# A two-layer diffusion backbone step: adaLN columns, W2 tile order, row splits and skewed output blocks

## The chip, the cores and the metric

The kernel runs on one core of a Trainium2 chip. The metric is the device time of one execution in microseconds (us). TensorE (PE) multiplies, VectorE (DVE), ScalarE (ACT) and GpSimd (POOL) do the elementwise work, and SyncE (SP) issues nearly all DMA transfers, in the order of its program.

## The reference

1152 tokens (1024 latent tokens and 128 context tokens) of width 1024 pass through two layers. Everything is float32.

```python
for i in range(2):
    sh1, sc1, g1, sh2, sc2, g2 = split(silu(cond) @ mod_w[i] + mod_b[i], 6)
    h = rmsnorm(x, norm1_g[i]) * (1 + sc1) + sh1
    if i == 0:    # gated short convolution
        bg, cg, xv = split(h @ sc_w_in, 3)
        y = (bg * dwconv3(cg * xv, conv_w, conv_b)) @ sc_w_out
    else:         # latent attention, 16 heads, with rotary keys and a context cache
        y = attention(h) @ mla_w_o
    x = x + g1 * y
    h = rmsnorm(x, norm2_g[i]) * (1 + sc2) + sh2
    x = x + g2 * (square(relu(h @ mlp_w1[i])) @ mlp_w2[i])
```

`cond` has two rows, one for the latent and one for the context tokens. It is the same for all tokens of its kind, so `mod` is a table of 96 columns (2 layers x 6 chunks x 8 tiles), each 128 x 2.

## The kernel before

Activations lie transposed: a tile is 128 channels x 1152 tokens, and `x`, `h_hi` and `h_lo` have eight tiles each. Every float32 operand is split into a high part (fp32r, a rounded copy) and a low part (the difference). `three` (line 845) makes each product as high x high, high x low and low x high, over three token blocks of 384 columns: nine matmuls for one tile of weights and one tile of rows.

A weight block is 128 x 1024. SP loads it into `w_raw`, ACT makes `w_hi` (line 532), POOL `w_lo` (line 459), in two slots that alternate. The high part of block b waits until PE has finished block b - 2. A stage is one output tile in three PSUM banks; there are two sets of banks, and `stage_free` counts how often one was read out. `stage` runs the eight tiles of one block. `skewed_blocks` runs two blocks in step, the second two tiles behind the first, so that PE has twice the work for each row tile as it comes. It is used behind a norm. `h_ready` makes PE wait for each low row tile.

The order of the work:

- Start. SP queues `vec`, `ident`, eight tiles of x, `mod_bias`, sixteen adaLN column tiles of 512 KB (`mod_first`), and then weight blocks (`load`) and adaLN rows (`load_mod`) in turn. PE copies the conditioning rows (`cond_rows`, line 913), makes columns 0 to 7 (`first_mod`, line 906), the sum of squares (lines 935 and 941) and columns 8 to 15. `first_mod_out` on DVE adds the bias. `norm` needs all sixteen: DVE scales x (line 1293), ACT adds the shift for the high part (line 562), DVE makes the low part (line 1305).
- Input blocks, 24 of them, three for each of eight channel tiles. DVE multiplies two outputs into `pad` (line 1422), filters it (lines 1428 and 1431) and multiplies by the third output (line 1439) into `v32`. In between it makes the next adaLN columns (`mod_next`, line 1241, two row products with an accumulator, and line 1244).
- `split_rows` on ACT (line 570) makes the high rows of `v32`, all eight behind the last product. `low_rows` on DVE (line 1315) makes the low rows.
- `out_blocks`: eight output blocks in a loop of pairs. DVE adds each to x (`residual`, line 1324), ACT squares, DVE adds the squares (line 1265).
- MLP: eight chunks. A chunk has four blocks of W1, each of which gives one hidden tile (ACT line 591, DVE line 1353, ACT line 594, DVE line 1358), and four blocks of W2. A W2 block gives two output tiles (halves) from four hidden tiles. PE runs half 0 over tiles 0 to 3 and then half 1. In the first W2 block (k == HT) half 0 waits for each hidden tile.
- Layer 1: latent projections, then eight pairs of heads. A step (`STEPS` is 19 for a head) is `scores` on PE, the exponential on ACT (line 767), its high part on ACT (line 769), its low part `p_lo` on POOL (line 475), `values` on PE. `over_sums` on DVE (lines 1664 and 1666) divides `o32` by the sums of a pair in five pieces. It does so in the middle of the next pair, and for the last pair behind it. The tiles `h_hi` and `h_lo` share memory with the latents and the heads' operands.
- Then `split_rows(o32)`, `low_rows`, the transfer that brings x back (queued on SP behind `sums_used`), `out_blocks`, norm, MLP.

Of the kernel before, what the change touches and what calls it, by code (L numbers as in the profile page):

```python
# [13 lines left out]
P = 128  # L14
# [36 lines left out]
SKEW = 2  # L51

# [96 lines left out]
def build(nc, T, outs):  # L149
    y_t, new_ckv, new_kpe = outs  # L150
    with ExitStack() as ctx:
# [30 lines left out]
        mod_acc = new("mod_acc", [P, 2, 2])  # L182
        gain = new("gain", [P, 4, KT, 2])
# [18 lines left out]
        mod_first0 = at("mod_first0", [P, KT, WSLOT], F32, G0)  # L202
# [8 lines left out]
        mod_first1 = at("mod_first1", [P, KT, WSLOT], F32, H0 + KT * N * 4)  # L211
# [56 lines left out]
        mod_prod = ps[:, 6 * BANK:8 * BANK]  # L268

# [16 lines left out]
        mf_loaded = [sem(f"mf_loaded{s}") for s in range(FIRST_MODS)]  # L286
# [25 lines left out]
        h_lo_done = sem("h_lo_done")  # L312
        relu_done = sem("relu_done")
# [33 lines left out]
        def _(sp):  # L347
# [24 lines left out]
            for j in range(KT):  # L372
                sp.dma_start(x[:, j, :], T["x_t"][:, j, :]).then_inc(x_loaded[j], 16)
            sp.dma_start(mod_bias[:, :], T["mod_bias"]).then_inc(const_in, 16)
            for m in range(FIRST_MODS):
                tile = (mod_first0, mod_first1)[m // KT]
                sp.dma_start(tile[:, m % KT, :], T["mod_cols"][m]).then_inc(mf_loaded[m], 16)
# [7 lines left out]
            load_in(0, 0)  # L385
# [132 lines left out]
        def _(act):  # L518
# [48 lines left out]
            def split_rows(src):  # L567

                for j in range(KT):
                    act.activation(h_hi[:, j, :], src[:, j, :], ACT.Copy).then_inc(h_hi_done, 1)  # L570

# [47 lines left out]
            act.wait_ge(row_mm, 1)  # L619
            act.activation(cond_row[:, :, :].rearrange("p c n -> p (c n)"), ps[:, 0:2 * D], ACT.Copy).then_inc(row_out, 1)  # L620

            def x_tile(j):
                act.wait_ge(x_loaded[j], 16)
                return x[:, j, :]

            rms(x_tile, KT, D)
            split_hi()
            split_hi()
            norm(0, 0, False)

            def in_blocks():

                for k in range(6):
                    if k % 3 == 0:
                        act.wait_ge(stage_done, L.count("s", 1))
                        act.wait_ge(stage_free, L.count("s"))
                        act.activation(cols3(tmp[0][:, 0:N]), stage_ps(L.at["s"]), ACT.Copy).then_inc(stage_free, 1)
                    L.at["s"] += 1
                    split_hi()

            with act.Fori(0, KT // 2) as i:
                L.enter(i, b=6, s=6)
                in_blocks()
                L.leave(KT // 2)
            act.wait_ge(stage_free, L.at["s"])
            split_rows(v32)
# [3 lines left out]
            if LAYERS > 1:  # L650
# [177 lines left out]
                act.wait_ge(sums_used, 3 + 3 * PAIRS)  # L828
                split_rows(o32)
# [6 lines left out]
        def _(pe):  # L836
# [11 lines left out]
            def stage(w0, tiles, src, ready=None):  # L848
# [5 lines left out]
                for k in range(tiles):  # L854
                    if ready:
# [4 lines left out]
                                [lambda t, r=r: r[:, k, t * TB:(t + 1) * TB] for r in src])  # L860
                ins.then_inc(stage_done, 1)
# [28 lines left out]
            def h_block(ready=None):  # L890
                weights()
                stage(lambda k: k * P, KT, (h_hi, h_lo), ready)
# [5 lines left out]
            def first_mod(m):  # L898

                b = 6 + m % 2  # L900
                raw = (mod_first0, mod_first1)[m // KT][:, m % KT, :]
                pe.wait_ge(mf_loaded[m], 16)
                if m >= 2:
                    pe.wait_ge(mod_done, m - 1)
                for k in range(KT):
                    ins = pe.matmul(bank(b, 2), raw[:, k * P:(k + 1) * P], cond[:, k, :], start=k == 0, stop=k == KT - 1)
# [38 lines left out]

            def chunk(behind_norm=None):
# [3 lines left out]
                for k in range(2 * HT):  # L950
                    if k < HT:
                        if not (behind_norm and k < 2):
                            h_block()
                    else:
                        weights()
                        for half in range(2):
                            def hid_ready(t):
                                pe.wait_ge(hid_lo_done, L.count("hid", -t - 1))
                            stage(lambda t: t * 2 * P + half * P, HT, (hid_hi, hid_lo),
                                  hid_ready if k == HT and half == 0 else None)  # L960
# [24 lines left out]
            with pe.Fori(1, KT // 2) as i:  # L985
# [3 lines left out]
                L.leave(KT // 2 - 1)  # L989
            C["h"] = KT  # L990

            def out_blocks():
                with pe.Fori(0, KT // 2) as i:
                    L.enter(i, b=2, s=2)
                    for k in range(2):
                        h_block(h_ready(C["h"]) if k == 0 else None)
                    L.leave(KT // 2)
# [220 lines left out]
        def _(dve):  # L1218
# [9 lines left out]
            def first_mod_out(m):  # L1228

                dve.wait_ge(mod_mm, m + 1)  # L1230
                dve.tensor_scalar(mod[:, m, :], bank(6 + m % 2, 2), mod_bias[:, m:m + 1], None,
                                  ALU.add).then_inc(mod_done, 1)
                L.at["m"] += 1

# [33 lines left out]
            def inverse_root():  # L1268
# [5 lines left out]
                dve.wait_ge(stage_free, L.at["s"])  # L1274
# [35 lines left out]
            def low_rows(dst, src, hi, n):  # L1310

                for j in range(n):
# [81 lines left out]
            for j in range(KT):  # L1394
                add_square(j % 2)
                first_mod_out(j)
            inverse_root()
            for m in range(KT, FIRST_MODS):
                first_mod_out(m)
            norm(0, 0, False)  # L1400
# [9 lines left out]
            with dve.Fori(0, KT // 2) as i:  # L1410
                L.enter(i, s=6, m=6)
                S.enter(i, n=12)
                for f in range(2):
                    mod_next(i * 6 + (FIRST_MODS + 3 * f))
                    L.at["s"] += 1

                    dve.wait_ge(stage_done, L.count("s", 1))
                    dve.wait_ge(stage_free, L.count("s"))
                    dst = [pad[:, 1:1 + 2 * TB].rearrange("p (t n) -> p t n", t=2),
                           pad[:, 1 + 2 * TB:1 + NS], pad[:, NS + 3:N + 3]]  # L1420
                    for o, (v, g, _) in zip(dst, parts(L.at["s"], tmp[0])):
                        ins = dve.tensor_tensor(o, v, g, ALU.mult)
                    ins.then_inc(stage_free, 1)
                    L.at["s"] += 1
                    mod_next(i * 6 + (FIRST_MODS + 3 * f + 1))
                    dve.wait_ge(stage_free, L.count("s"))
                    col = [vec[:, ds(i * 2 + (taps + w * KT + f), 1)] for w in range(3)]
                    own(dve.tensor_scalar(tmp[2][:, 0:W2], pad[:, 0:W2], col[0],
                                          vec[:, ds(i * 2 + (bias0 + f), 1)], ALU.mult, ALU.add))
                    for w in (1, 2):  # L1430
                        own(dve.scalar_tensor_tensor(tmp[2][:, 0:W2], pad[:, w:w + W2], col[w], tmp[2][:, 0:W2],
                                                     ALU.mult, ALU.add))

                    dve.wait_ge(stage_done, L.count("s", 1))
# [381 lines left out]
```

## Time and profile before

| | |
|---|---|
| median of 3 runs | 3251.74 us (3251.46 to 3254.78) |
| profiled execution | 3250.7 us, span 3248.9 us |
| PE busy | 3053.8 us (94%) |
| DVE, ACT, POOL busy | 1478.2, 1009.9, 852.4 us |
| mean granted PE clock | 0.959 of full speed |

Times in the rows are microseconds from the start of the span. A line of the timeline gives start, duration, engine, line, operation, output and inputs, the count, and in brackets how long the engine had been idle and what ended that. The granted clock is either 1.0 (2.4 GHz) or 0.5 (1.2 GHz) at any moment; a stretch shows the mean.

### The profile page before, as it was taken

To read this page: it belongs to the slowest core of one execution; us is meant where nothing else is said; L and a number is where in the kernel's file an instruction comes from. 1 tells how busy PE (TensorE), PEld (TensorE's weight loads), DVE (VectorE), ACT (ScalarE), POOL (GpSimd) and SP (SyncE) were. 2 spreads that over 40 slices of the span, in tenths; PEclk is the share of its full clock that TensorE was granted. 3 is DMA by queue.
4 is the path that set the end of the run, shared out by engine and by line. 5 is a ranking of instruction groups with operands and counts; after the bars stand their busy time and mean duration, and the time that the engine had idled before them with its cause. 6 is when DMAs were issued, how large, how long until landed. Compare 5 with 4: busy or idle time off the path is not lost.

```text
span 3248.9 us, 43718 instructions
## 1 busy us (share of the span) xinstructions
PE 3053.8 (94%) x17193; PEld 2920.4 (90%) x17193; DVE 1478.2 (45%) x1856; ACT 1009.9 (31%) x1447; POOL 852.4 (26%) x509
## 2 busy tenths in 40 slices
PE   7999998999999999887999999999889999999999
PEld 7999998999999999886777787777789999999999
DVE  1654545555445555744566565665433222222222
ACT  2211213111111112222766677766422111111111
POOL 0121111221121211120544456545311112121211
PEclk6999998999999999886999999999989999999999
DMA  5222220222112221120000000000211111111112
GB/s 196 67 78 93 75 90 33 78 85 72 64 65 89 79 71 58 59 73 6 8 7 2 7 5 7 8 6 1 88 35 33 46 39 40 44 45 39 39 45 78
DMA packets 45532, 166.60 MB, mean 51 GB/s; under 512 B 5792, under 2 KB 7456, under 8 KB 45216
## 3 DMA queue, kind: packets, MB, share of 16 engines
q1 hardware_dynamic: 44912, 160.89, 14.2%
q10 hardware_dynamic: 560, 4.87, 0.4%
q8 instruction: 43, 0.70, 0.1%
q14 instruction: 17, 0.14, 0.0%
HBM read 156.15 MB, written 9.58 MB: 51 GB/s over the span
## 4 chain that ended last, share of the span: by engine, by line
PE 49%; issue 33%; POOL 12%; DVE 3%; ACT 2%; POOLq 0%; DVEq 0%; ACTq 0%
PE ps L845 48%; POOL p_lo L475 10%; POOL w_lo L459 2%; DVE tmp L1353 1%; DVE hid_lo L1358 1%; ACT hid_hi L594 1%; ACT tmp L591 1%; DVE x L1324 0%; DVE ps L1241 0%; PE ps L941 0%; ACT tmp L539 0%; PE ps L935 0%; DVE tmp L1265 0%; ACT p L767 0%; POOLq L474 0%
## 5 line engine op out<-in xcount | busy, mean ns | idle before, releaser
L459 POOL TENSOR_TENSOR w_lo<-w_raw,w_hi 128x1024 fp32r<-128x1024 f32 (+2 forms) x190 | 462.5, 2434 | 1978.0 <-ACT w_hi L532 1978.0
L845 PE MATMUL ps<-h_hi,w_hi 128*128 128x384 f32 x2640 | 607.4, 338 | 49.7 <-DVE h_lo L1305 24.8
L845 PE MATMUL ps<-h_lo,w_hi 128*128 128x384 f32 x2640 | 604.3, 336 | 0.0
L845 PE MATMUL ps<-h_hi,w_lo 128*128 128x384 f32 x2640 | 603.5, 336 | 0.0
L845 PEld LDWEIGHTS ps<-h_hi,w_hi 128*128 128x128 f32 x2640 | 474.4, 190 | 54.1 <-issue 43.7
L532 ACT ACTIVATE w_hi<-w_raw 128x1024 fp32r<-128x1024 f32 (+2 forms) x190 | 194.6, 1025 | 984.3 <-PE ps L845 912.1
L475 POOL TENSOR_TENSOR p_lo<-p,p_hi 128x512 fp32r<-128x512 f32 (+1 forms) x304 | 381.7, 1270 | 375.9 <-ACT p_hi L769 372.5
L845 PEld LDWEIGHTS ps<-h_lo,w_hi 128*128 128x128 f32 x2640 | 475.2, 190 | 0.0
L845 PEld LDWEIGHTS ps<-h_hi,w_lo 128*128 128x128 f32 x2640 | 474.5, 189 | 0.0
L1324 DVE SCALAR_TENSOR_TENSOR x<-ps,mod,x 128x256 f32<-128x256 f32 (+5 forms) x432 | 240.1, 612 | 480.2 <-PE ps L845 478.6
L845 PE MATMUL ps<-hid_hi,w_hi 128*128 128x384 f32 x1536 | 350.4, 335 | 9.7 <-DVE hid_lo L1358 9.6
L845 PE MATMUL ps<-hid_lo,w_hi 128*128 128x384 f32 x1536 | 348.8, 334 | 0.0
L845 PE MATMUL ps<-hid_hi,w_lo 128*128 128x384 f32 x1536 | 348.7, 334 | 0.0
L1353 DVE SCALAR_TENSOR_TENSOR tmp<-ps,tmp 128x1152 f32<-128x1152 f32 x64 | 86.9, 1358 | 494.4 <-ACT tmp L591 494.4
L845 PEld LDWEIGHTS ps<-hid_hi,w_hi 128*128 128x128 f32 x1536 | 272.5, 188 | 15.1 <-DVE hid_lo L1358 14.7
L845 PEld LDWEIGHTS ps<-hid_hi,w_lo 128*128 128x128 f32 x1536 | 273.8, 188 | 0.0
L845 PEld LDWEIGHTS ps<-hid_lo,w_hi 128*128 128x128 f32 x1536 | 273.7, 188 | 0.0
L1646 DVE TENSOR_REDUCE row_max<-ps 128x1 f32<-128x1152 f32 x144 | 178.1, 1237 | 155.5 <-PE ps L1118 155.5
L591 ACT ACTIVATE tmp<-ps 128x1152 f32<-128x1152 f32 x64 | 72.6, 1135 | 531.7 <-PE ps L845 531.7
L767 ACT ACTIVATE p<-ps 128x512 f32<-128x512 f32 (+1 forms) x304 | 175.7, 578 | 119.5 <-PE ps L845 111.3
L1241 DVE CUSTOM_DVE_ANT_0 ps<-mod_raw,cond_row 128x1024 f32<-128x1024 f32 x80 | 211.6, 2645 | 1.6 <-issue 0.7
L769 ACT ACTIVATE p_hi<-p 128x512 fp32r<-128x512 f32 (+1 forms) x304 | 187.0, 615 | 9.7
(135 smaller groups left out, 3567.1 us busy)
## 6 DMA issues: line engine op xcount, KB each, us to landing
w_raw<-in_wall_dram SPq DMA_DIRECT2D x174, 512.0 KB, 3.7
mod_raw<-in_mod_rows_dram SPq DMA_DIRECT2D x80, 512.0 KB, 3.5
mod_first<-in_mod_cols_dram SPq DMA_DIRECT2D x16, 512.0 KB, 15.0
x<-in_x_t_dram SPq DMA_DIRECT2D x8, 576.0 KB, 7.4
x_spill<-x ACTq DMA_DIRECT2D x1, 4608.0 KB, 15.3
x<-x_spill SPq DMA_DIRECT2D x1, 4608.0 KB, 13.5
out_dram<-x SPq DMA_DIRECT2D x8, 576.0 KB, 2.8
w_raw<-in_wall_dram SPq DMA_DIRECT2D x8, 416.0 KB, 3.1
```

Of the source, the lines that this page charges most:

```text
L459: pool.tensor_tensor(w_lo[s][:, 0:words], w_raw[s][:, 0:words], w_hi[s][:, 0:words].bitcast(F32), ALU.subtract).then_inc(w_lo_done, 1)
L475: pool.tensor_tensor(p_lo[s][:, 0:n], p32[s][:, 0:n], p_hi[s][:, 0:n].bitcast(F32), ALU.subtract).then_inc(p_lo_done, 1)
L532: act.activation(w_hi[s][:, 0:words], w_raw[s][:, 0:words], ACT.Copy).then_inc(w_hi_done, 1)
L591: act.activation(cols3(tmp[0][:, 0:N]), stage_ps(L.at["s"]), ACT.Relu).then_inc(relu_done, 1)
L594: act.activation(hid_hi[:, k, :], tmp[1][:, 0:N], ACT.Copy).then_inc(hid_hi_done, 1)
L767: act.activation(p32[s][:, 0:n], bank(3 + pos % 2, n), ACT.Exp, scale=SCALE).then_inc(p_exp, 1)
L769: act.activation(p_hi[s][:, 0:n], p32[s][:, 0:n], ACT.Copy).then_inc(p_hi_done, 1)
L845: ins = pe.matmul(out, lhs[a], rhs[b](cols), start=first and n == 0, stop=last and n == 2)
L1241: ins = dve.tensor_tensor_reduce(product, raw, cond_row[:, c, :], 1.0, 0.0, ALU.mult, ALU.add, mod_acc[:, slot, c:c + 1])
L1324: ins = dve.scalar_tensor_tensor(xt, v, mod[:, ds(gate, 1), c:c + 1].rearrange("p a c -> p (a c)"), xt, ALU.mult, ALU.add)
L1353: dve.scalar_tensor_tensor(cols3(tmp[1][:, 0:N]), stage_ps(L.at["s"]), 0.0, cols3(tmp[0][:, 0:N]), ALU.max, ALU.mult).then_inc(stage_free, 1)
L1646: dve.tensor_reduce(row_max[:, t:t + 1], ps[:, 0:n], AX_X, ALU.max).then_inc(max_free, 1)
```

## The change

Four things are changed.

1. Start. Only the eight shift columns are made on PE (`first_shift`), three ahead of the sum of squares and five behind it. The scale columns come as rows (`scale_rows`) and are made on DVE as `mod_next` makes the later ones (`first_gain`, straight into `gain`). `mod_bias` is queued ahead of x. The column tiles, weight blocks 0 and 1 and the scale rows are queued among the tiles of x and behind them. ACT squares two tiles ahead of copying the conditioning rows, and splits weight blocks 0 and 1 ahead of the root.
2. `first_down_block` runs the first W2 block of each chunk in the order of `DOWN_ORDER`.
3. Convolution result: in the last input block PE signals `h_free` behind each tile of `h`, ACT splits `v32` tiles 0 to 6 behind these, and DVE makes their low rows ahead of the last product. Tile 7 follows behind it. Attention result: DVE makes the high rows of tiles 0 to 6 and the low rows of tiles 0 to 4 during the last pair, and the rest behind the sums. ACT does none of it.
4. `out_blocks` begins with `skewed_blocks` for its first two blocks, in both layers.

```diff
+ROWS_FREE = 5
+FIRST_SHIFTS, FIRST_GAINS = 3, 2
+DOWN_ORDER = [(0, 0), (0, 1), (0, 2), (1, 0), (1, 1), (0, 3), (1, 2), (1, 3)]
...
+            sp.dma_start(mod_bias[:, :], T["mod_bias"]).then_inc(const_in, 16)
...
+            for j in range(0, KT, 2):
+                load_x(j)
+                load_x(j + 1)
+                load_shift(j // 2)
+            load(0)
+            load(1)
+            for k in range(KT // 2):
+                load_scale(k)
+                load_shift(KT // 2 + k)
+            for k in range(KT // 2, KT):
+                load_scale(k)
...
-            load_in(0, 0)
+            load_mod(0)
+            load_mod(1)
+            load(2)
+            load_mod(2)
...
-            rms(x_tile, KT, D)
+                square(x[:, j, :], j % 2, D)
             split_hi()
             split_hi()
+            rms(None, 0, D)
+            act.wait_ge(mod_done, FIRST_MODS)
             norm(0, 0, False)
...
-            act.wait_ge(stage_free, L.at["s"])
-            split_rows(v32)
+            act.wait_ge(stage_free, L.at["s"] - 3)
+            for j in range(KT):
+                if j < KT - 1:
+                    act.wait_ge(h_free, j + 1)
+                else:
+                    split_hi()
+                    act.wait_ge(stage_free, L.at["s"])
+                act.activation(h_hi[:, j, :], v32[:, j, :], ACT.Copy).then_inc(h_hi_done, 1)
...
+            def first_down_block():
+
+                weights()
+                slot = L.at["b"] % 2
+                for half, t in DOWN_ORDER:
+                    if t == 0:
+                        pe.wait_ge(stage_free, L.count("s", 1 - half))
+                    if half == 0:
+                        pe.wait_ge(hid_lo_done, L.count("hid", -t - 1))
...
-            for m in range(KT):
-                first_mod(m)
+            for k in range(FIRST_SHIFTS):
+                first_shift(k)
             pe.wait_ge(row_out, 1)
             sum_squares(KT)
-            for m in range(KT, FIRST_MODS):
-                first_mod(m)
+            for k in range(FIRST_SHIFTS, KT):
+                first_shift(k)
...
             def out_blocks():
-                with pe.Fori(0, KT // 2) as i:
+                skewed_blocks(h_ready(C["h"]))
+                with pe.Fori(1, KT // 2) as i:
...
+            def first_gain(k):
+
+                dve.wait_ge(scale_loaded[k], 16)
+                raw, slot = mod_scale[:, k, :], k % 2
+                for c, product in enumerate((mod_junk[:, :], raw)):
+                    ins = dve.tensor_tensor_reduce(product, raw, cond_row[:, c, :], 1.0, 0.0, ALU.mult, ALU.add,
+                                                   mod_acc[:, slot, c:c + 1])
+                own(ins)
+                g0 = VEC["norm1_g"][0]
+                dve.tensor_scalar(gain[:, 0, k, :], mod_acc[:, slot, :], scale_bias[:, k:k + 1],
+                                  vec[:, g0 + k:g0 + k + 1], ALU.add, ALU.mult).then_inc(mod_done, 1)
...
+                for k in range(KT):
+                    if k == FIRST_GAINS:
+                        inverse_root(False)
+                    first_gain(k)
+                dve.wait_ge(stage_free, L.at["s"])
+                scaled(0)
+                shifts_out()
...
+                if last:
+                    low_rows(h_lo, v32, h_hi, 0, KT - 1)
+                dve.wait_ge(stage_done, L.count("s", 1))
...
+                def high_row(j):
+                    dve.tensor_copy(h_hi[:, j, :], o32[:, j, :]).then_inc(h_hi_done, 1)
+
                 pair(False, True, PAIRS - 2)
+                dve.wait_ge(sums_used, 3 * PAIRS)
+                for j in range(ROWS_FREE):
+                    high_row(j)
+                    low_rows(h_lo, o32, h_hi, j, j + 1)
+                for j in range(ROWS_FREE, KT - 1):
+                    high_row(j)
                 for piece in range(5):
                     over_sums(piece, PAIRS - 1)
                 dve.wait_ge(sums_used, 3 + 3 * PAIRS)
-                low_rows(h_lo, o32, h_hi, KT)
+                low_rows(h_lo, o32, h_hi, ROWS_FREE, KT - 1)
+                high_row(KT - 1)
+                low_rows(h_lo, o32, h_hi, KT - 1, KT)
```

## Rows read from the trace of the kernel before

**Rows 1.** The page, part 1: busy time, share and instructions of each engine.

```profile
PE 3053.8 (94%) x17193; PEld 2920.4 (90%) x17193; DVE 1478.2 (45%) x1856; ACT 1009.9 (31%) x1447; POOL 852.4 (26%) x509
```

**Rows 2.** Waits on PE: total us, times, the longest.

```profile
PE ps L845 <- DVE h_lo L1315: 19.1, 2, 11.4
```

**Rows 3.** Stretches: length, busy PE, PEld, DVE, ACT, POOL, clock, DMA share, GB/s.

```profile
16.00:22.10 6.10, 5.98 (x32) 5.98 (x32) 0.00 (x0) 0.00 (x0) 0.00 (x0) 1.00 1.03 410
...
55.70:80.40 24.70, 24.67 (x131) 24.58 (x129) 1.54 (x7) 3.02 (x3) 4.65 (x2) 0.56 0.07 22
...
581.03:681.76 100.73, 100.14 (x576) 99.82 (x576) 51.38 (x63) 17.25 (x16) 20.32 (x9) 1.00 0.21 74
...
2272.00:2289.00 17.00, 16.55 (x70) 12.60 (x69) 0.03 (x1) 15.89 (x29) 15.18 (x12) 1.00 0.00 0
...
2309.66:2315.10 5.44, 5.44 (x17) 5.44 (x18) 5.44 (x5) 5.44 (x6) 0.00 (x0) 0.51 1.00 434
```

**Rows 4.** Timeline of the start, up to the first DVE row products.

```profile
16.12 6.25 PE L913 MATMUL ps<-ident,cond 128*128 128x128 f32 x32 [16.12 <-DMA mod_bias<-in_mod_bias_dram]
...
52.16 3.78 PE L941 MATMUL ps<-ident,root 128*128 128x128 f32 x18 [0.61 <-DVE root L1272]
...
55.78 24.59 PE L906 MATMUL ps<-cond,mod_first 128*128 128x2 f32 x128
...
80.41 0.22 DVE L1231 TENSOR_SCALAR mod<-ps,mod_bias 128x2 f32<-128x2 f32 x1 [3.19 <-PE ps L906]
...
85.69 1.30 PE L845 MATMUL ps<-h_hi,w_hi 128*128 128x384 f32 x3 [5.32 <-DVE h_lo L1305]
...
105.90 1.23 DVE L1241 CUSTOM_DVE_ANT_0 ps<-mod_raw,cond_row 128x1024 f32<-128x1024 f32 x1 [0.28 <-DVE tmp L1406]
...
108.58 0.23 DVE L1244 TENSOR_SCALAR mod<-mod_acc,mod_bias 128x2 f32 x1 [0.30 <-DVE mod_acc L1241]
```

**Rows 5.** Timeline of the convolution seam.

```profile
385.13 1.42 DVE L1431 SCALAR_TENSOR_TENSOR tmp<-tmp,vec,tmp 128x1154 f32<-128x1154 f32 x1 [0.15 <-DVE tmp L1431]
...
388.94 1.49 DVE L1439 TENSOR_TENSOR v<-ps,tmp 128x768 f32 x3 [2.38 <-PE ps L845]
389.87 2.35 POOL L459 TENSOR_TENSOR w_lo<-w_raw,w_hi 128x1024 fp32r<-128x1024 f32 x1 [10.02 <-ACT w_hi L532]
...
394.84 10.24 DVE L1315 TENSOR_TENSOR h_lo<-v,h_hi 128x1152 fp32r<-128x1152 f32 x8
...
396.34 1.30 PE L845 MATMUL ps<-h_hi,w_hi 128*128 128x384 f32 x3 [7.64 <-DVE h_lo L1315]
```

**Rows 6.** Timeline of DVE in the first W2 block of a chunk, layer 0.

```profile
585.77 1.66 DVE L1324 SCALAR_TENSOR_TENSOR x<-ps,mod,x 128x768 f32<-128x768 f32 x3
```

**Rows 7.** Timelines of SP, PE and DVE at the attention seam.

```profile
2306.89 0.33 SPq L432 DMA_DIRECT2D x<-x_spill  x1
...
2309.66 1.30 PE L845 MATMUL ps<-h_hi,w_hi 128*128 128x384 f32 x3 [11.41 <-DVE h_lo L1315]
...
2320.71 1.02 DVE L1258 MEMSET tmp<- 128x1152 f32 x1 [2.31 <-DMA x<-x_spill]
```

**Rows 8.** Timelines of DVE and POOL where operations on SBUF meet.

```profile
382.53 0.88 DVE L1428 TENSOR_SCALAR tmp<-tmp,vec 128x1154 f32<-128x1154 f32 x1
...
694.12 2.10 DVE L1244 TENSOR_SCALAR mod<-mod_acc,mod_bias 128x2 f32 x1 [0.18 <-DVE mod_acc L1241]
...
692.80 3.40 POOL L459 TENSOR_TENSOR w_lo<-w_raw,w_hi 128x1024 fp32r<-128x1024 f32 x1 [8.85 <-ACT w_hi L532]
...
1572.01 1.04 DVE L1616 TENSOR_TENSOR q_tok<-q_tok,r_tok 128x864 f32<-128x864 f32 x1
...
1572.42 1.79 POOL L475 TENSOR_TENSOR p_lo<-p,p_hi 128x512 fp32r<-128x512 f32 x1 [0.45 <-ACT p_hi L769]
...
2300.93 2.34 POOL L459 TENSOR_TENSOR w_lo<-w_raw,w_hi 128x1024 fp32r<-128x1024 f32 x1 [3.57 <-ACT w_hi L532]
2301.02 2.53 DVE L1666 TENSOR_TENSOR o<-o,sums 128x256 f32<-128x256 f32 x1
```

More of the change, by code:

```diff
@@ L846, in three, with stage @@
                 return ins
-            def stage(w0, tiles, src, ready=None):
+            def stage(w0, tiles, src, ready=None, free=None):
                 s, slot = L.at["s"], L.at["b"] % 2
@@ L860, in stage @@
                                 [lambda t, r=r: r[:, k, t * TB:(t + 1) * TB] for r in src])
+                    if free and k < tiles - 1:
+                        ins.then_inc(free, 1)
                 ins.then_inc(stage_done, 1)
@@ L896, in h_ready, with first_shift @@
                 return lambda k: pe.wait_ge(h_lo_done, base + k + 1)
[L898 to L906, printed above, removed]
+            def first_shift(k):
+                pe.wait_ge(shift_loaded[k], 16)
+                for j in range(KT):
+                    ins = pe.matmul(shift_ps[:, 2 * k:2 * k + 2], mod_shift[:, k, j * P:(j + 1) * P], cond[:, j, :],
+                                    start=j == 0, stop=j == KT - 1)
                 ins.then_inc(mod_mm, 1)
@@ L944, in sum_squares @@
                 L.at["s"] += 1
+            def first_down_block():
[6 more added lines that the diff above has]
+                        pe.wait_ge(hid_lo_done, L.count("hid", -t - 1))
+                    v = stage_ps(L.at["s"] + half)
+                    w = t * 2 * P + half * P
+                    ins = three([(v[:, c, :], c) for c in range(3)], t, t == 0, t == HT - 1,
+                                [w_hi[slot][:, w:w + P], w_lo[slot][:, w:w + P]],
+                                [lambda c, h=h: h[:, t, c * TB:(c + 1) * TB] for h in (hid_hi, hid_lo)])
+                    if t == HT - 1:
+                        ins.then_inc(stage_done, 1)
+                L.at["s"] += 2
+                L.at["b"] += 1
             def chunk(behind_norm=None):
@@ L956, in chunk @@
                         for half in range(2):
[L957 to L960, printed above, removed]
+                            stage(lambda t: t * 2 * P + half * P, HT, (hid_hi, hid_lo))
                         L.at["b"] += 1
@@ L1308, in norm, with low_rows @@
                     ins.then_inc(h_lo_done, 1)
-            def low_rows(dst, src, hi, n):
-                for j in range(n):
+            def low_rows(dst, src, hi, first, end):
+                for j in range(first, end):
                     C["h"] += 1
@@ L1395, in _ @@
                 add_square(j % 2)
[L1396 to L1400, printed above, removed]
+            first_norm()
             pad = tmp[1]
```

173 lines of the change are left out of this document (105 added, 68 removed).

## The prediction

> **What bounds the kernel now.** I read the page first: TensorE (PE) is busy for 3053.8 us of 3248.9 [rows 1], so a saving must remove PE idle time or time at a low granted clock, and no other engine's share matters by itself. The list of waits on PE then names the candidates: two waits for the low rows of line 1315 make 19.1 us [rows 2]. I then took a table of stretches and the timeline around each place that the diff touches.
>
> Start: PE sits still until 16.12, because the copies of the conditioning rows wait for a semaphore that also counts `mod_bias`, which is queued behind 4.7 MB of x. Then come sixteen column products at 3.41 us each, and the first real matmul is at 85.69 [rows 4]. The queue moves 410 GB/s there [rows 3].
>
> Convolution seam: the input blocks end at 388.70 and the first output block starts at 396.34, 7.64 us later [rows 5]. Its first three matmuls take 1.30 us, as at the attention seam [rows 7], where the clock is 0.51 [rows 3]: PE has fallen to 1.2 GHz. Here the full clock is back at 400.1, so half of 3.8 us is lost as well, 1.8 by the matmuls made; together 9.4.
>
> MLP: one chunk takes 100.73 us for 576 matmuls [rows 3]. Without a wait they take 0.520 us per three, as their loads do (99.82 in that row), 99.84 in all, so 0.89 us per chunk is the wait for the last hidden tile. There are sixteen chunks.
>
> Attention seam: PE waits 11.41 us for line 1315, up to 2309.66 [rows 7], then runs 5.4 us at clock 0.51 [rows 3], another 2.7 us lost: 14.1 in all.
>
> **Part 1, the start.** `mod_bias` goes ahead of x, so the conditioning rows run from about 4.1 (when `cond` is ready; the constants have landed by then at the same early rate as `vec` and `ident`) to 10.4, by their 6.25 us [rows 4]. Eight shift columns stay on PE, three ahead of the sum of squares, five behind; the eight scale columns become two row products and a gain on VectorE (DVE), each 2.9 us (105.90 to 108.81) [rows 4]. By 0.41 MB/us [rows 3] and the new order of the queue, x is in at 19.1, the first two weight blocks at 21.7 and 23.0, and the scale rows at 24.2, 26.8, 29.4 and so on to 38: from the second on they come faster than DVE uses them. DVE: last square added at 21.8; first gain from 24.2, but the two w_lo subtractions of GpSimd (POOL) run from 22.9, and each can hold up a DVE operation (see part 4), so I give the first gain 6.3 us, to 30.5; second gain to 33.4; reciprocal to 33.7. PE: broadcast of the root 3.8 us [rows 4] to 37.5, then five shift columns at 3.41 to 54.6. DVE's other six gains end at 51.3, and its first scaling at 52.9, so PE's columns set the end. Then shifts out, ScalarE (ACT) high part, DVE low part: 3.4 us, and the first block starts at 58.0. Before 85.69: **27.7 us gained.** Bounds: 31 if PE has its full clock in the five columns (the end is then DVE's), 24 if the gains are held up twice more. From here on all waits are as before.
>
> **Part 2, the convolution seam.** High rows are now split while the last input block still runs, tile by tile behind `h_free`, and the low rows stand in `in_group` ahead of the last product. But DVE is not free: its filter ends at 386.55 (385.13 + 1.42) [rows 5]. Seven low rows at 1.28 us (10.24 / 8) end at 395.5; ACT's split of block 25 still comes at 388.7, so POOL's 2.35 us w_lo falls among them: 397.9. Only then comes the last product, 1.49 us, and it is this product that frees the banks: 399.4. PE starts output block 24 at 388.70 at once, and needs these banks behind three tiles of 1.56 us, at 393.4. So a stall of 6.0 us takes the place of the 7.64, and the clock falls as in the old gap, 1.7. The last tile's low row (about 403.6) is not needed until PE has made nine more tiles, and hides. The skew costs one thing: the third block's weights can be split only when stage 24 is done, two tiles (3.1 us) ahead of need, against 1.06 + 2.40 and latency = 3.6: 0.5. Sum 9.4 - 6.0 - 1.7 - 0.5 = **1.2 gained**; bounds -1 and +5 (no collision with POOL, no fall of clock).
>
> **Part 3, W2 tile order.** The last hidden tile is now needed behind five tiles and not three, 3.1 us later than before; the wait is 0.89, so it goes: 16 x 0.89 = 14.2. What is late next: in layer 0 DVE reaches the first half's update only at 585.77, behind its adaLN product, and it takes 1.66 [rows 6]. This half is now finished at about 585.1 and its banks are needed at 588.2: 0.8 us to spare. The second half first needs the banks of the last hidden stage, which are free 2.6 us after that stage, ahead of 4.7. I take **13.8**; bounds 7 (layer 0 gives nothing) and 14.2.
>
> **Part 4, the attention seam.** Seven high rows and five low rows move from behind the last pair into it, on DVE. DVE is idle there, from 2271.7 to 2288.97, but POOL is busy 15.18 of 17.00 us [rows 3], making the p_lo that PE waits for. The trace shows that the two engines exclude each other on such operations: a 0.42 us product started at 2301.02 took 2.53, until POOL's subtraction from 2300.93 was over; and a POOL p_lo of 1.29 took 1.79 behind DVE's product of 1572.01 [rows 8]. One-input operations on SBUF do it too: a 0.23 us one [rows 4] took 2.10 beside w_lo [rows 8]. The nearest row to the new copy is the one-input operation over 1154 columns, 0.88 us [rows 8], some 0.75 of it transfer. So the shared port must carry, from 2271.9 to the last values, POOL's seventeen p_lo of 1.26 and a small one (21.8), and DVE's 7 x 0.75 + 5 x 1.25 = 11.5: 33.3, where 26.3 us pass now. That is 7.0 too much, and the steps don't pack perfectly: **8.3 later**. Bounds: 2 (copies take no share of the port), 12.5 (copies at 1.28 us that do).
>
> The Trainium skill (GPSIMD Engine Reference, section 1 Specifications) has this as contention of POOL's SBUF interface "with DVE instructions in a 2-port perf mode or with two SBUF inputs"; by its sister page (VectorE: DVE Perf Modes, the perf-mode tier table) an fp32 copy in SBUF runs at the doubled rate, which would put these copies under that rule. The rows above agree for a TENSOR_SCALAR; no row shows a copy.
>
> Behind the last values at T, PE starts output block tiles 0 to 4 at once. The second block's weights: w_lo at T + 5.1 (now 2303.27 [rows 8], with T at 2298.25) against T + 4.7, 0.5. The normalisation ends 8.6 us behind T as now (2306.89 [rows 7]), tiles 5 and 6 are low at T + 11.2 against a need at T + 13, hidden. But x comes back from memory 13.8 us behind that point (2320.71 [rows 7]), now T + 22.5, and the third block's weights land behind it at T + 23, w_lo at T + 26.6 against T + 25.7: 0.9. One short fall of the clock, 1.7. Sum 14.1 - 8.3 - 0.5 - 0.9 - 1.7 = **2.7 gained**; bounds -5 and +10.
>
> **Sum.** 27.7 + 1.2 + 13.8 + 2.7 = 45.4. The profiled execution took 3250.7 (span 3248.9), 1.0 under the median of the runs; so 3205.3, and for the median 3206.
>
> **Rivals.** (a) The moved row work hides after all: DVE finds gaps in POOL's work and the seams give nearly all: 8 more in part 4, 4 in part 2, so 3194. For it: PE, not POOL, paces the steps until 2289. Against: 33.3 us on a port in 26.3. Chance 0.2. (b) A moved edit turns into a full new wait: copies at one element per cycle with the port held, and a fallen clock in the last pair: 8 to 10 more, 3215. Chance 0.17. (c) The W2 order does nothing: the wait moves to the banks behind DVE's adaLN product, in both halves: 13.8 lost, 3220. Against: layer 1 has no such product. Chance 0.06. (d) Slower: in the last pair PE gets to work 60% of each step, its clock falls to 1.2 GHz and stays there through the output projection, as it stays low (0.56) all through the 24.7 us of the column products at the start [rows 3]. Eight blocks at half clock cost 99.8 us more; this decides once more than 45 us are lost, so if the low clock holds for over 90 us. Against: at both seams full work brought it back within 6 us [rows 3]. About 3280. Chance 0.02. The forecast as summed: 0.55.
>
> **Numbers.** Likeliest 3206. The range takes in (a), most of (b) and the bounds of part 1 (+3, -4): 3193 to 3219. No change from before can be told below 0.2%, 6.5 us. Faster 0.96, same 0.02, slower 0.02.
>
> **What would show it.** First block's matmul at 58 (52 to 61). In the convolution seam a gap three tiles into the output blocks, ended by the last product, about 6 us. Chunks of 99.9 us. In the last pair, p_lo of 1.5 to 2.5 us and DVE copies that do the same, with steps near 2 us; then no gap over 2 us at the attention seam. The prediction fails if p_lo stays at 1.29 there, if the start is bound by rows that land late, or if the chunks keep 100.7.

## The result, and the profile after

| | before | after |
|---|---|---|
| median, before run again beside after | 3252.31 us (3251.46 to 3254.78) | 3200.56 us (3199.45 to 3203.68), 4 runs |
| ratio | | 0.9841 (95% interval 0.9824 to 0.9858) |
| profiled execution | 3250.7, span 3248.9 | 3203.68, span 3201.9 |

The kernel became 1.6% faster. The forecast was 3206, with a range of 3193 to 3219. The profiled execution of after is the slowest of its four, 3.1 us above their median. A likely cause, the granted clock at the start, is told below.

The page of after, engines first and the granted PE clock in 40 slices second, against [rows 1]: PE is busy for 27.5 us less, and the span is 47.0 shorter.

```profile
PE 3026.3 (95%) x17065; PEld 2894.8 (90%) x17065; DVE 1517.1 (47%) x1889; ACT 1002.6 (31%) x1439; POOL 862.7 (27%) x509
...
PEclk6999999999999999886999999999989999999999
```

The list of waits on PE in after (total, times, longest). The first line is the waits for a low row behind a norm, which before has too. The sixteen waits for the low part of a hidden tile, which the same list of before has with 9.6 us (the line by itself), are gone. New are the one wait for `v` at line 1532 (5.4) and a part of those for `w_lo`, which are the convolution seam and the attention seam.

```profile
PE ps L875 <- DVE h_lo L1402: 20.3, 6, 6.0
...
PE ps L875 <- POOL w_lo L486: 7.7, 4, 2.9
...
PE ps L875 <- DVE v L1532: 5.4, 1, 5.4
```

```profile
PE ps L845 <- DVE hid_lo L1358: 9.6, 16, 0.7
```

I cut both traces at the same landmarks and subtracted. This table is the accounting that the rest works from.

| stretch | before | after | gained | forecast |
|---|---|---|---|---|
| start of the span to the first block's matmul | 85.69 | 58.73 | 27.0 | 27.7 |
| input blocks | 303.0 | 303.0 | 0.0 | 0 |
| convolution seam and its eight output blocks | 109.5 | 108.0 | 1.5 | 1.2 |
| norm and MLP of layer 0 | 833.9 | 827.2 | 6.7 | 6.9 |
| latents, to the first pair | 289.9 | 286.6 | 3.3 | 0 |
| pairs of heads but the last | 596.4 | 600.7 | -4.3 | 0 |
| last pair, head 0 | 50.7 | 49.3 | 1.4 | 0 |
| last pair, head 1 | 27.8 | 33.3 | -5.5 | -8.3 |
| attention seam and output blocks | 115.3 | 103.7 | 11.6 | 11.0 |
| norm and MLP of layer 1 | 836.7 | 831.3 | 5.4 | 6.9 |

**Start.** The timeline of after, start and duration in us, answers to [rows 4]. PE does its five late columns from 38.11 to 55.2, behind the root's broadcast (34.11). DVE's first gain is at 25.58, and its first scaling at 50.56. PE then waits 3.55 us for the first low row, and the first block starts at 58.73.

```profile
3.82 6.10 PE L942 MATMUL ps<-ident,cond 128*128 128x128 f32 x32 [3.82 <-DVE cond L1487]
...
25.58 1.88 DVE L1291 CUSTOM_DVE_ANT_0 mod_junk<-mod_scale,cond_row 128x1024 f32<-128x1024 f32 x1 [2.56 <-DMA mod_scale<-in_scale_rows_dram]
...
34.11 4.21 PE L970 MATMUL ps<-ident,root 128*128 128x128 f32 x18 [7.10 <-DVE root L1368]
38.11 17.07 PE L934 MATMUL ps<-cond,mod_shift 128*128 128x2 f32 x80
...
50.56 1.55 DVE L1306 SCALAR_TENSOR_TENSOR tmp<-x,gain,rstd 128x1024 f32<-128x1024 f32 x2
...
58.73 1.30 PE L875 MATMUL ps<-h_hi,w_hi 128*128 128x384 f32 x3 [3.55 <-DVE h_lo L1326]
```

**Convolution seam.** The same view around the end of the input blocks, against [rows 5]. DVE makes seven low rows from 359.13 to 370.3, POOL's `w_lo` (362.97, 3.57 instead of 2.4) among them. Only then comes the last product (370.21), which frees the banks. PE has stood still for 5.41 us by 371.83, and its next matmuls take 1.30: the low clock.

```profile
359.13 11.16 DVE L1412 TENSOR_TENSOR h_lo<-v,h_hi 128x1152 fp32r<-128x1152 f32 x7
362.97 3.57 POOL L486 TENSOR_TENSOR w_lo<-w_raw,w_hi 128x1024 fp32r<-128x1024 f32 x1 [10.07 <-ACT w_hi L559]
370.21 1.47 DVE L1532 TENSOR_TENSOR v<-ps,tmp 128x768 f32<-128x768 f32 x3
371.83 1.30 PE L875 MATMUL ps<-h_hi,w_hi 128*128 128x384 f32 x3 [5.41 <-DVE v L1532]
```

**Last pair and attention seam.** In the last head POOL's nineteen `p_lo` form one chain of 32.59 us without a gap, 1.72 us each in the mean. In before the same nineteen take 23.97 us in five pieces with gaps between them (the second view shows one piece: 1.30 each). DVE's copies (CAST) and subtractions stand in it at 1.8 and 2.3 us each. The same copy alone at 2279.45, when POOL is idle, takes 0.75. At the seam PE waits 0.38 at 2273.33 where it waited 11.41 [rows 7], and a wait of 1.5 for a `w_lo` follows with the third block. x comes back at 2290.69.

```profile
2234.72 32.59 POOL L502 TENSOR_TENSOR p_lo<-p,p_hi 128x512 fp32r<-128x512 f32 x19 [0.73 <-ACT p_hi L801]
...
2236.20 1.82 DVE L1813 CAST h_hi<-o 128x1152 fp32r<-128x1152 f32 x1
2238.05 2.35 DVE L1412 TENSOR_TENSOR h_lo<-o,h_hi 128x1152 fp32r<-128x1152 f32 x1
2240.32 1.83 DVE L1813 CAST h_hi<-o 128x1152 fp32r<-128x1152 f32 x1
...
2273.33 0.79 PE L875 MATMUL ps<-h_hi,w_hi 128*128 128x384 f32 x3 [0.38 <-POOL w_lo L486]
...
2279.45 0.75 DVE L1813 CAST h_hi<-o 128x1152 fp32r<-128x1152 f32 x1
...
2290.69 1.02 DVE L1354 MEMSET tmp<- 128x1152 f32 x1 [9.09 <-DMA x<-x_spill]
```

```profile
2282.59 6.51 POOL L475 TENSOR_TENSOR p_lo<-p,p_hi 128x512 fp32r<-128x512 f32 x5 [0.45 <-ACT p_hi L769]
```

**Stretches.** The columns are the stretch and its length, then busy us (and instructions) of PE, PE's weight loads, DVE, ACT and POOL, then the granted clock, the DMA share and GB/s. First the late columns (clock 0.50 throughout), then 5.8 us behind the convolution seam (0.53), then the last head (1.00, POOL busy 32.68 of 33.5), then 100 us of each MLP, in which PE is not idle at all, against 99.82 of 100.73 for its loads in [rows 3].

```profile
38.11:55.20 17.09, 17.07 (x81) 16.98 (x80) 13.43 (x25) 1.13 (x1) 0.00 (x0) 0.50 0.26 102
...
371.83:377.60 5.77, 5.77 (x19) 5.77 (x20) 5.28 (x8) 1.05 (x1) 0.00 (x0) 0.53 0.39 118
...
2233.50:2267.00 33.50, 28.48 (x112) 18.93 (x110) 31.92 (x20) 25.20 (x44) 32.68 (x21) 1.00 0.00 1
...
553.00:653.00 100.00, 100.00 (x579) 100.00 (x578) 51.29 (x63) 17.26 (x16) 20.59 (x9) 1.00 0.22 74
2500.00:2600.00 100.00, 100.00 (x578) 100.00 (x578) 24.21 (x32) 17.25 (x16) 20.47 (x9) 1.00 0.14 43
```

### The profile page after: what moved, and what is told of

Read it like the earlier page. It is cut to its first block, busy times and chain, and to the rows that moved or that the text cites. A ratio compares the mean times of both kernels' runs of the same rounds, so it can differ in the third digit from the quotient of the medians.

```text
span 3201.9 us, 43418 instructions
## 1 busy us (share of the span) xinstructions
PE 3026.3 (95%) x17065; PEld 2894.8 (90%) x17065; DVE 1517.1 (47%) x1889; ACT 1002.6 (31%) x1439; POOL 862.7 (27%) x509
## 4 chain that ended last, share of the span: by engine, by line
PE 51%; issue 32%; POOL 13%; DVE 2%; ACT 1%; POOLq 0%; DVEq 0%; ACTq 0%
PE ps L875 51%; POOL p_lo L502 11%; POOL w_lo L486 2%; DVE x L1421 0%; DVE ps L1337 0%; PE ps L970 0%; ACT tmp L566 0%; PE ps L964 0%; DVE tmp L1361 0%; POOLq L501 0%; DVE h_lo L1402 0%; DVE mod_raw L1337 0%; PE ps L1169 0%; DVE ql_lo L1412 0%; DVE sums L1765 0%
## 5 line engine op out<-in xcount | busy, mean ns | idle before, releaser
L502 POOL TENSOR_TENSOR p_lo<-p,p_hi 128x512 fp32r<-128x512 f32 (+1 forms) x304 | 390.6, 1300 | 374.0 <-ACT p_hi L801 370.8
## 6 DMA issues: line engine op xcount, KB each, us to landing
x_spill<-x ACTq DMA_DIRECT2D x1, 4608.0 KB, 13.8
```

The costliest lines, as they stand in the source:

```text
L502: pool.tensor_tensor(p_lo[s][:, 0:n], p32[s][:, 0:n], p_hi[s][:, 0:n].bitcast(F32), ALU.subtract).then_inc(p_lo_done, 1)
```

## The experiments

Medians are set beside the 3200.56 of after and the 3251 to 3252 of before, which ran again on each chip. Where a difference is of a few us I also go by landmarks inside the profiled execution. For the convolution seam that is one distance: from the first block's matmul to DVE's update of x behind the last output block. It is 412.84 in before (85.69 to 498.53) and 411.39 in after (58.73 to 470.12), and it doesn't contain the start or anything of the attention. The kernels below that leave this seam alone show how far to trust it: 412.54 and 412.71 in the other two with the old seam, and 410.18, 410.68, 410.93 and 410.98 in the other four with the new one. So after's is the longest of its five, and the distance says nothing below 1.2 us.

**1. W2 order alone, in the kernel before.**

```diff
+DOWN_ORDER = [(0, 0), (0, 1), (0, 2), (1, 0), (1, 1), (0, 3), (1, 2), (1, 3)]
...
                     elif k == HT:
+                        first_down_block()
```

> The kernel before with only the order of the first W2 block changed. Theory (the wait for the last hidden tile goes and nothing takes its place): chunks of 99.84 us in both layers, 16 x 0.89 = 14 us off, about 3238. Rival (the banks behind VectorE's adaLN product hold PE in layer 0): chunks of 100.7 in layer 0 and 99.84 in layer 1, 7 us off. Granted clock at other places may shift it by 2 to 4 us either way.

Measured: 3238.7 (3236.44 to 3238.96), ratio 0.9962 (0.9948 to 0.9976), 12.4 us under before. PE has no idle time in 100 us of either MLP (stretches of layer 0 and layer 1 below).

```profile
580.00:680.00 100.00, 100.00 (x578) 100.00 (x578) 51.34 (x64) 17.26 (x16) 20.79 (x9) 1.00 0.22 74
2486.00:2586.00 100.00, 100.00 (x579) 100.00 (x578) 24.36 (x33) 17.25 (x16) 20.60 (x9) 1.00 0.13 43
```

So layer 0 gives its share too, although DVE reaches the first half's update late there, behind its adaLN product; the rival that the banks take over the wait fails. What is left of it is one wait of 0.8 us for DVE's update of x in the whole kernel (one of 0.5 in after).

**2. Convolution seam: three low rows ahead of the last product, four behind it.**

```diff
+ROWS_AHEAD = 3
...
-                    low_rows(h_lo, v32, h_hi, 0, KT - 1)
+                    low_rows(h_lo, v32, h_hi, 0, ROWS_AHEAD)
...
+                if last:
+                    low_rows(h_lo, v32, h_hi, ROWS_AHEAD, KT - 1)
```

> The changed kernel with three low rows of the convolution result ahead of the last product and four behind it. Theory (the product that frees the banks stands behind seven low rows): the product ends near 364.7 in place of 371.7, the 5.4 us gap three tiles into the output blocks goes, and the short fall of the clock behind it with it: 7 us off the changed kernel, about 3194. Rival (PE would wait there for the second block's low weights or for the low rows anyway): a gap of 3 us or more stays, less than 3 us off.

Measured: 3191.99 (3191.59 to 3193.55), ratio 0.9822 (0.9806 to 0.9838): 8.6 under after, and its slowest run is under the fastest of after. PE has no wait at all in this seam and keeps its clock (1.00 from 355 to 385). The first block is at 55.41, the last update at 458.62, so the distance is 403.21, 8.2 less than in after and at least 7.0 less than in any kernel with its seam. The timeline of DVE:

```profile
355.81 3.90 DVE L1413 TENSOR_TENSOR h_lo<-v,h_hi 128x1152 fp32r<-128x1152 f32 x3
359.62 1.48 DVE L1533 TENSOR_TENSOR v<-ps,tmp 128x768 f32<-128x768 f32 x3
361.02 6.05 DVE L1413 TENSOR_TENSOR h_lo<-v,h_hi 128x1152 fp32r<-128x1152 f32 x4
```

The product now ends at 361.1, against 371.7 in after, or 368.4 if both are counted from the first block, and each of the four late rows is in time for PE. Together with the 1.45 us that after had gained, the seam gives 9.6 against before, the whole of the 9.4 that the forecast had found in it. So it was the order of DVE's work that had given the gain back, and not its amount.

**3. One gain ahead of the root instead of two.** `FIRST_SHIFTS, FIRST_GAINS = 3, 2` becomes `3, 1`.

> The changed kernel with one gain ahead of the reciprocal of the root and not two. Theory (PE's five shift columns behind the broadcast set the start; VectorE's gains have 3.2 us to spare there): the broadcast begins 2.7 us sooner, near 31.4, and the first block 2 to 3 us sooner, where VectorE takes over as the bound. Rival (VectorE's gains set it): first block where it was, for the same granted clock.

Measured: 3199.9 (3198.09 to 3201.78), ratio 0.984 (0.9824 to 0.9857): nothing gained. The root came 2.6 us sooner, as meant, but the first block did not:

```profile
31.54 3.77 PE L970 MATMUL ps<-ident,root 128*128 128x128 f32 x18 [4.35 <-DVE root L1368]
35.15 14.36 PE L934 MATMUL ps<-cond,mod_shift 128*128 128x2 f32 x80
...
55.62 1.30 PE L875 MATMUL ps<-h_hi,w_hi 128*128 128x384 f32 x3 [6.12 <-DVE h_lo L1326]
```

The columns took 14.36 us here and not 17.07 (clock 0.60), so PE was granted the full clock for a part of them; then it waited 6.12 for DVE, and not 3.55. DVE's chain of gains sets the start when the clock rises. The six other kernels with the changed start and two gains had their first block at 55.4 to 55.8 in their profiled executions, with columns of 13.95 to 14.47 us. In these six PE's columns and DVE's first scaling end within 0.1 us of each other.

The profiled executions of after and of the first kernel in experiment 8, which has one gain as well, had clock 0.50 all through the columns. This pair tests the theory at equal clock. The timeline of the latter:

```profile
35.58 17.07 PE L935 MATMUL ps<-cond,mod_shift 128*128 128x2 f32 x80
...
56.20 1.30 PE L876 MATMUL ps<-h_hi,w_hi 128*128 128x384 f32 x3 [3.55 <-DVE h_lo L1327]
```

Its first block comes 2.5 us sooner than the 58.73 of after, as the theory says. So, by one profiled execution of each kernel, one gain ahead of the root helps where the clock stays low, and is worth nothing where it rises.

**4. Nine of the row operations of the last pair in its head 0.** One operation follows each maximum of head 0.

```diff
+                        if last:
+                            row_step(t)
...
-                for j in range(ROWS_FREE):
-                    high_row(j)
-                    low_rows(h_lo, o32, h_hi, j, j + 1)
+                for n in range(NT, 2 * ROWS_FREE):
+                    row_step(n)
```

> The changed kernel with nine of VectorE's row operations moved from head 1 to head 0 of the last pair, one behind each maximum. Theory (the delay is port time beside a saturated GpSimd; in head 0 GpSimd is busy half of the time and VectorE idle 1.3 us of each 2.6): head 1's stretch falls from 33.3 to 28.5 to 30, head 0's grows by at most 2, so 2 to 4 us off the changed kernel. Rival (the maxima are late behind the row operations and PE waits for them): head 0 grows by 4 us or more, nothing gained.

Measured: 3196.36 (3194.24 to 3197.64), ratio 0.9828 (0.9812 to 0.9845), 4.2 under after. Head 1 takes 28.5 us (33.3 in after, 27.8 in before), head 0 takes 49.7 (49.3 in after). In head 0 five of the nine run undisturbed, and there a copy takes 0.74, a subtraction 1.35; three subtractions (2.1) and a copy (1.6) met POOL, the last line is one of them.

```profile
2202.27 0.74 DVE L1774 CAST h_hi<-o 128x1152 fp32r<-128x1152 f32 x1
...
2204.61 1.35 DVE L1412 TENSOR_TENSOR h_lo<-o,h_hi 128x1152 fp32r<-128x1152 f32 x1
...
2211.38 2.12 DVE L1412 TENSOR_TENSOR h_lo<-o,h_hi 128x1152 fp32r<-128x1152 f32 x1
```

So 4.8 of the 5.5 us that head 1 lost came back for 0.4 in head 0: they were the price of doing this work in head 1, where POOL is never idle.

**5. The seven copies made twice.** It tells what one more such operation costs.

```diff
+            if j < KT - 1:
+                own(dve.tensor_copy(h_hi[:, j, :], o32[:, j, :]))
             own(dve.tensor_copy(h_hi[:, j, :], o32[:, j, :]))
```

> The changed kernel with each of the seven VectorE copies in the last pair made twice (same output). Theory (VectorE and GpSimd exclude each other on the port to SBUF, and a copy holds it for about 0.6 us): the stretch from the end of head 0's p_lo to the last p_lo grows from 33.3 by 7 x 0.6 = 4 us, less what slack is left (3 to 5), to 36.5 to 38.5; added copies take 1.8 us each where p_lo runs. Rival (the delay is not the port but the number of steps in which VectorE is late): the stretch stays at 33.3, since nothing in it waits for VectorE.

Measured, in one execution (3203.48): the chain of `p_lo` grows from 32.59 to 34.77, by 2.2, and each copy beside it takes 1.7 to 1.8 (the last two, behind its end, 1.0 and 0.8). I had expected 3 to 5.

```profile
2230.68 34.77 POOL L502 TENSOR_TENSOR p_lo<-p,p_hi 128x512 fp32r<-128x512 f32 x19 [0.75 <-ACT p_hi L801]
...
2232.17 1.80 DVE L1814 CAST h_hi<-o 128x1152 fp32r<-128x1152 f32 x1
2234.01 1.73 DVE L1815 CAST h_hi<-o 128x1152 fp32r<-128x1152 f32 x1
```

The size fits how the engines alternate: behind each `p_lo` one waiting DVE operation passes. There are nineteen `p_lo`, so more operations on DVE can delay only those that had none ahead of them. By an estimate from these traces they are four to six, and the third operation of a group adds 0.5 us (a group of three starts every 5.88 us here, three `p_lo` alone take 3.9, and a pair costs 1.54). This is argued from the spacing, and no run tests it by itself.

**6. Five reciprocals more in the same place**, of 128 columns, whose results nothing uses. A reciprocal has one input and its duration (0.95 for 128 columns) is far longer per column than a copy's (0.75 for 1152), so it is not one that runs at the copy's rate.

```diff
                 for j in range(ROWS_FREE):
+                    own(dve.reciprocal(rstd[:, 0:P], o32[:, j, 0:P]))
                     high_row(j)
```

> The changed kernel with five reciprocals of 128 columns (0.95 us each, 4.7 us of VectorE time, one input, not in a doubled rate) put among the row work of the last pair; their result is not used. Theory (only operations that hold the port delay p_lo): p_lo goes on as before during a reciprocal, and the stretch from the end of head 0's p_lo to the last p_lo stays at 33.3 or falls a little, 32 to 33.8. Rival (any VectorE work there delays the steps): grows by 3 to 5 us like the doubled copies.

Measured, in one execution (3196.97): the chain is 32.59 us again, to the hundredth.

```profile
2228.11 32.59 POOL L502 TENSOR_TENSOR p_lo<-p,p_hi 128x512 fp32r<-128x512 f32 x19 [0.74 <-ACT p_hi L801]
...
2229.59 0.95 DVE L1818 RECIPROCAL rstd<-o 128x128 f32<-128x128 f32 x1
2230.58 0.84 DVE L1813 CAST h_hi<-o 128x1152 fp32r<-128x1152 f32 x1
```

The reciprocal at 2229.59 ran in the midst of a `p_lo`, neither delayed nor delaying, and the copy behind it then waited for less (0.84 instead of 1.8). So DVE being busy does not by itself cost POOL anything; the copies and the two-input subtractions do. For the copies alone experiment 5 shows it, for the two together experiment 4.

The Trainium skill (GPSIMD Engine Reference, section 1 Specifications) names two kinds that contend with POOL, a DVE instruction "in a 2-port perf mode or with two SBUF inputs". The trace agrees for the subtractions, which have two inputs (2.33 beside a `p_lo`, 1.35 alone). For the copies it agrees if they are in such a mode; that they take 0.75 for as many columns fits it, but no run here shows the mode.

**7. The skew taken out of both `out_blocks`**, all else as in after.

```diff
-                skewed_blocks(h_ready(C["h"]))
+                for k in range(2):
+                    h_block(h_ready(C["h"]) if k == 0 else None)
```

> The changed kernel without the skew of the output blocks. Theory: at the convolution seam the skew is what makes PE need the freed banks three tiles in; without it banks are needed eight tiles in (12.5 us) and the last low row, made 13.8 us behind the last input block, is needed seven tiles in (10.9): a wait of 3 us in place of 5.4 and 0.6. At the attention seam tile 5 is made 10 us behind the last values and needed at 7.9: a wait of 2 in place of 0.4 and 1.5. So the skew costs 2 to 4 us in sum; 3197. Rival (the skew is what hides the rows): without it the waits grow by 3 us or more at each seam, 3206.

Measured: 3196.6 (3194.93 to 3199.29), ratio 0.9828 (0.9811 to 0.9844), 4.0 under after; the two intervals overlap. The landmarks decide: 55.81 to 463.85 is 408.04, so 3.35 us of it lie in the convolution seam (2.1 to 3.35 against the five kernels with the skew and late rows). The list of waits on PE there, 350 to 400:

```profile
PE ps L875 <- DVE h_lo L1413: 2.8, 1, 2.8
```

One block at a time uses one set of banks for its eight tiles, so the set that the last product frees isn't wanted for 12.5 us, and PE waits for a row (2.8) instead of the banks (5.4). The skew costs there. At the attention seam the waits are 2.3 without the skew against 0.4 + 1.5 with it, hardly a difference.

**8. The row edits of 2 and 4 together, with and without the skew.** The first also has the one gain of experiment 3.

> All three edits together: three low rows ahead of the convolution product, one gain ahead of the reciprocal, nine row operations in head 0. If the three causes are separate the gains add: 7 + 2.5 + 3 = 12 us off the changed kernel, about 3188; granted clock may move it by 3 either way.

> The two row edits (three low rows ahead of the convolution product, nine row operations in head 0), two gains as in the changed kernel, and no skew of the output blocks. With the rows early enough neither form should wait much: convolution seam 1.5 us against 0 with skew, attention seam 2.3 us against 2.0. So 1 to 3 us behind the kernel with all three edits, 3188 to 3190.

Measured: with the skew 3187.13 (3185.41 to 3187.47), ratio 0.9799 (0.9783 to 0.9815), 13.4 under after and the best of all; without it 3191.22 (3186.34 to 3193.18), ratio 0.9811 (0.9794 to 0.9827). The distance over the convolution seam is 403.21 with the skew (56.20 to 459.41) and 405.16 without (55.54 to 460.70). So the skew's sign depends on the rows: it costs 2.1 to 3.35 us when they and the banks are late, and gains 1.95 when they are in time. The list of waits on PE from 350 to 400 is empty with the skew and has 1.3 us for low rows without it, as PE has two blocks of work for each row with it. The gain rests on one profiled execution of each kernel.

**9. Only `mod_bias` ahead of x, in the kernel before.** Its one line `sp.dma_start(mod_bias[:, :], T["mod_bias"])` moves from behind x to behind `ident`.

> The kernel before with only the transfer of the adaLN bias moved ahead of x. It splits the gain of the start. Theory (PE's chain of sixteen columns sets the start, and its first column then waits for data behind x, near 16.5 in place of 22.2): first block 5 to 6 us sooner, near 80, so 3246, and the other 21 of the 27 us come from the eight columns that left PE. Rival (most of the gain is the early start of PE itself): first block 12 us sooner, 3240.

Measured: 3250.52 (3246.9 to 3253.57, ten runs), ratio 0.9994 (0.9985 to 1.0004). Nothing was gained, which neither theory had expected. The conditioning rows do run at 3.73, twelve us sooner than in [rows 4], but PE then idles for 8.31 us until the first column tile lands, and makes all sixteen columns at the low clock: 27.4 us for eight, where before makes eight in 24.59 [rows 4]. Timeline of PE, then the stretch 14 to 89 (clock 0.50, where before has 0.59):

```profile
17.60 27.47 PE L906 MATMUL ps<-cond,mod_first 128*128 128x2 f32 x128 [8.31 <-DMA mod_first<-in_mod_cols_dram]
53.52 27.31 PE L906 MATMUL ps<-cond,mod_first 128*128 128x2 f32 x128
86.15 1.30 PE L845 MATMUL ps<-h_hi,w_hi 128*128 128x384 f32 x3 [5.32 <-DVE h_lo L1305]
```

```profile
14.00:89.00 75.00, 65.46 (x301) 65.18 (x301) 20.28 (x35) 15.66 (x17) 4.67 (x2) 0.50 0.39 154
```

So an early bias by itself is worth nothing in the kernel before. By elimination the start's gain comes from the rest of the edit, above all, I think, from the eight scale columns that leave PE: made there, eight columns take 27.3 us at the low clock. No run takes the early bias out of the changed kernel, so what it is worth there is not known.

## Why the prediction was right, point by point

The forecast of 3206 lies 5.4 above the median, inside the range, and the case named as likeliest is what happened. By parts, the profiled executions give 27.0 + 1.5 + 12.1 + 6.1 = 46.7, where 27.7 + 1.2 + 13.8 + 2.7 = 45.4 were forecast; the untouched stretches add 0.4 (3.3 - 4.3 + 1.4).

**Part 1, the start: right, and the bound was nearer than the term.** The broadcast came at 34.11 and not at 33.7, the columns took 17.07 (forecast 17.1), the last stretch 3.55 (3.4). But the low clock through all five columns, which I took as the term, is what two profiled executions in nine of the changed start showed. In the seven others the columns took 14 to 14.5 us and the first block is at 55.4 to 55.8; with 55.6 that is 30.1 us gained, near the bound "31 if PE has its full clock", though the clock was full for a part of the columns only. The working had the sign of this in its rows: it gives all sixteen columns of before 3.41 us each, but the second eight took 24.59 together, 3.07 each, at clock 0.56 [rows 3]. That the term fits the profiled execution so well is in part luck. The low clock puts the profiled execution of after some 3 us above its own other runs (3203.68 against a median of 3200.56). That those runs had a higher clock in the columns is argued from the other kernels' profiles, not shown.

**Part 2, the convolution seam: right in mechanism, and the size by terms that cancel.** The stall is 5.4 (forecast 6.0), ended by the last product. The fall of the clock behind it costs 2.6 (forecast 1.7): six groups of three matmuls take 5.70 us from 371.83 on, and 3.12 at full clock. The wait of 0.5 for the third block's weights did not come. Experiment 2 shows the cause. The sentence that failed is "The skew costs one thing", 0.5: by experiment 7 the skew costs 2.1 to 3.35 us here. The forecast sum had this within the stall without naming it: it is only with two blocks in step that PE needs the product's banks "behind three tiles". I had priced the seam right and put its price on the product alone. The 1.5 gained is itself the least of its kind, since the four other kernels with this seam have a distance shorter by 0.4 to 1.2.

**Part 3, the W2 order: mechanism right, size 12.1 to 12.4 for 13.8.** The wait is gone in both layers. The norms and MLPs gave 6.7 and 5.4, where 6.9 each was forecast. In layer 1 a short stretch at the low clock (2421.34 to 2426.15), which before did not have, takes 1.7 of it.

**Part 4, the attention seam: 6.1 for 2.7.** The exclusion of POOL and DVE is what the trace and experiments 5 and 6 show; rival (a), that the row work hides, and rival (b), that it costs 8 to 10 more, both fail. The term that was mis-sized is "33.3, where 26.3 us pass now", and with it the 8.3. I added a copy (0.75) and a subtraction (1.25) to the port in full. The timeline of DVE in after shows a copy and a subtraction every 4.12 us (2236.20 to 2240.32 above), and two `p_lo` pass in that time. Alone these two take 2.58, so the pair of operations costs 1.54 and not 2.0. Five pairs and two more copies make about 8.7 in place of 11.5, which is the 2.8 between 8.3 and the measured 5.5. Also the fall of the clock (1.7) did not come: PE never stood still for more than 1.5 us at this seam, and the granted clock is 1.00 from 2266.9 to 2290. The two small waits, 0.4 and 1.5, were forecast as 0.5 and 0.9. With these the seam would have gained 12.2 where it gained 11.6; 0.6 stays unexplained.

**Rivals (c) and (d).** Experiment 1 refutes (c). The clock in the last head was 1.00, so (d) had no ground.

**What stays open.** The pairs of heads before the last took 4.3 us longer in the profiled execution of after, and the latents 3.3 less, with the same instructions and no new kind of wait; the granted clock differs (0.98 against 0.97 for the pairs, 0.81 against 0.83 for the latents). Which short waits of PE the low clock follows differs between executions: behind the same wait of 2.90 us for `w_lo` in the MLP of layer 1 it came in after (2421.34) and not in before (2462.75). No run here isolates why. It limits what a profiled execution can say of a single stretch to 3 or 4 us. Also open is what each of the edits at the start is worth, since only the bias and the number of gains were tried by themselves.

## What to carry to other kernels

When work is moved into an idle stretch of an engine, look at the order inside that stretch: the one operation that frees something for the bottleneck engine goes first, and only then the work that has time. An engine's idle time is also not free where another engine's chain holds their common path to SBUF: place copies and two-input operations of VectorE where GpSimd is idle. A schedule that interleaves two blocks needs both sets of buffers early, so it pays only once the buffers and rows are in time.

## What the runs showed of the hardware that was not expected

- Between two queued GpSimd subtractions of 512 columns exactly one waiting VectorE operation passes. Seven more VectorE copies lengthened a chain of nineteen by only 2.2 us, while the copies beside it took 1.8 us instead of 0.75.
- A reciprocal of 128 columns (0.95 us) ran beside the same chain with no effect on either, and the chain was 32.59 us in both kernels.
- With the conditioning rows twelve us earlier, PE made the same sixteen columns in 27.4 + 27.3 us at clock 0.50: after an idle time of 8.3 us PE worked on them nearly without a gap, and the granted clock stayed at 1.2 GHz through both stretches. What an earlier start gave (the first column 4.6 us sooner), the lower clock took.
